# First two weight units unit by unit, later loads and clears reordered, last gate units by column halves

## What is computed

```
def reference(x, p, ...):
    h = x
    for i in range(DEPTH):                                  # DEPTH = 2
        h = h + 0.5 * swiglu(rmsnorm(h, ffn1_norm[i]), ffn1_w_gate[i], ffn1_w_up[i], ffn1_w_down[i])
        z = rmsnorm(h, mix_norm[i]) @ w_in[i]
        ...                                                 # short convolution and S5 scan over z give y
        h = h + y @ w_out[i]
        h = h + 0.5 * swiglu(rmsnorm(h, ffn2_norm[i]), ffn2_w_gate[i], ffn2_w_up[i], ffn2_w_down[i])
        gate = jax.nn.sigmoid(rmsnorm(h, ple_norm[i]) @ ple_w_gate[i])
        h = h + (p[i] @ ple_w_proj[i]) * gate
    return rmsnorm(h, final_norm)
```

## Times and profile before

| what | us |
|---|---|
| three executions | 1086.29, 1085.98, 1090.78 |
| their median | 1086.29 |
| the profiled execution | 1091.05 |
| its span in the trace | 1089.2 |
| TensorE busy | 1050.0 (96%) |
| VectorE busy | 675.1 (62%) |
| ScalarE busy | 513.1 (47%) |
| GpSimd busy | 408.0 (37%) |
| all TensorE waits for VectorE's `uL` (L933) | 10.9, in 2 places |
| TensorE waits for GpSimd's issue (L1296), at the start | 4.9, in 1 place |

### The profile page before, as it was taken

The page is one execution under the profiler, slowest core; times in us unless marked ns, Lnnn a source line. Parts: engine busy times, 40 slices in busy tenths (PEclk is TensorE's granted clock), DMA queues, the critical chain, the costliest instruction groups (busy, mean ns, idle before and its releaser), DMA issues.

```text
span 1089.2 us, 15176 instructions
## 1 busy us (share of the span) xinstructions
PE 1050.0 (96%) x5353; PEld 897.4 (82%) x5353; DVE 675.1 (62%) x772; ACT 513.1 (47%) x696; POOL 408.0 (37%) x605
## 2 busy tenths in 40 slices
PE   6999999999979999999999999999997999999996
PEld 5888888899877888888878888889997888888885
DVE  4555666468976555764777555546698765545464
ACT  4544444473364444444564444435535544444453
POOL 5888999314415888970029300001071100000000
PEclk9999999988989999999999999999798999999998
DMA  9655555241335955555536555552323465555541
GB/s 271 209 181 190 193 193 181 90 158 75 116 103 171 259 191 171 189 195 190 187 123 212 195 180 186 192 192 77 117 78 104 149 211 193 193 190 184 185 156 39
DMA packets 143385, 181.55 MB, mean 167 GB/s; under 512 B 18352, under 2 KB 125552, under 8 KB 143344
## 3 DMA queue, kind: packets, MB, share of 16 engines
q1 hardware_dynamic: 143200, 180.48, 50.3%
q10 hardware_dynamic: 144, 0.52, 0.1%
HBM read 179.93 MB, written 1.05 MB: 166 GB/s over the span
## 4 chain that ended last, share of the span: by engine, by line
PE 84%; DVE 11%; ACT 2%; issue 1%; SPq 1%; DMA 0%; POOL 0%; POOLq 0%; DVEq 0%; ACTq 0%
PE ps L1333 26%; PE ps L1335 26%; PE ps L1334 25%; DVE wL L706 2%; PE ps L1435 2%; PE ps L1345 1%; PE ps L1574 1%; PE ps L1575 1%; DVE regT L848 1%; ACT bufB L550 1%; DVE regT L835 1%; DVE bufA L871 1%; DVE regE L843 1%; PE ps L1451 1%; DVE uL L854 1%
## 5 line engine op out<-in xcount | busy, mean ns | idle before, releaser
L706 DVE TENSOR_TENSOR wL<-raw,wH 128x1024 fp32r<-128x1024 f32 x336 | 429.3, 1320 | 137.8 <-ACT wH L396 137.4
L396 ACT ACTIVATE wH<-raw 128x1024 fp32r<-128x1024 f32 x336 | 335.4, 1051 | 169.1 <-PE ps L1335 161.7
L1333 PE MATMUL ps<-wH,uH 128*128 128x512 f32 x832 | 330.2, 397 | 3.0 <-DVE uL L733 1.6
L1335 PE MATMUL ps<-wH,uL 128*128 128x512 f32 x832 | 324.6, 390 | 0.0
L1334 PE MATMUL ps<-wL,uH 128*128 128x512 f32 x832 | 324.4, 390 | 0.0
L1333 PEld LDWEIGHTS ps<-wH,uH 128*128 128x128 f32 x832 | 156.5, 188 | 36.0 <-DVE uL L733 3.6
L1335 PEld LDWEIGHTS ps<-wH,uL 128*128 128x128 f32 x832 | 156.3, 188 | 33.2
L1334 PEld LDWEIGHTS ps<-wL,uH 128*128 128x128 f32 x832 | 156.6, 188 | 30.8
L1068 POOL TENSOR_SCALAR ms<-ssq 128x2 f32<-128x2 f32 x8 | 4.5, 566 | 439.2 <-ACT bufB L410 409.7
L1333 PE MATMUL ps<-wH,hTH 128*128 128x512 f32 x352 | 140.1, 398 | 0.0
L1335 PE MATMUL ps<-wH,hTL 128*128 128x512 f32 x352 | 137.6, 391 | 0.0
(11 more groups left out here) (172 smaller groups left out, 1232.1 us busy)
## 6 DMA issues: line engine op xcount, KB each, us to landing
raw<-in_ffn_w_down_dram SPq DMA_DIRECT2D x88, 512.0 KB, 3.9
raw<-in_ffn_w_gate_dram SPq DMA_DIRECT2D x87, 512.0 KB, 4.0
raw<-in_ffn_w_up_dram SPq DMA_DIRECT2D x87, 512.0 KB, 5.0
raw<-in_w_in_dram SPq DMA_DIRECT2D x32, 512.0 KB, 4.3
raw<-in_w_out_dram SPq DMA_DIRECT2D x16, 512.0 KB, 4.0
raw<-in_ple_w_gate_dram SPq DMA_DIRECT2D x16, 512.0 KB, 3.7
raw<-in_glu_w_dram SPq DMA_DIRECT2D x4, 512.0 KB, 3.6
raw<-in_ple_w_proj_dram SPq DMA_DIRECT2D x4, 512.0 KB, 3.8
```

What stands on the lines that cost most here:

```text
L396: nc.scalar.activation(wH[:, slot, w], raw[:, slot, w], ACT.Copy).then_inc(wh_done, 1)
L706: nc.vector.tensor_tensor(wL[:, slot, w], raw[:, slot, w], wH[:, slot, w].bitcast(F32), ALU.subtract).then_inc((wl_half, wl_done)[a], 1)
L1333: mul(o, sH, vH, start=start, stop=False)
L1335: return mul(o, sL, vH, start=False, stop=stop)
```

## The change

1. **Start, TensorE.** In layer 0, tile 1 of x is transposed right behind tile 0, on its load's own semaphore, with six more warming products after it. Then unit 0 is used for both tiles, then unit 1 for both (`very_first_gate_up`), then the vectors are transposed.
2. **Start, VectorE and ScalarE.** The quarters are normed in the order 0, 2, 1, 3 (`norm_turn`). VectorE splits both halves of unit 0 behind quarter 0, and the halves of unit 1 around the rest of quarter 3; ScalarE splits unit 1 after all four quarters. The split of unit 2 comes ahead of the first silu.
3. **Start, loads and clears.** Tile 1 of x is loaded by SyncE, ahead of the second half of unit 0. The couplings are issued behind unit 4 instead of ahead of unit 3. GpSimd clears `regE` first, `Gr` and `Gi` behind the loads of x, `taps` and the vectors' step behind the first inverse norm.
4. **Parameters, both layers.** The three groups of `turn_params` stand together between the two tiles of unit 3, in PSUM banks 7, 2 and 3, without a wait between them; TensorE waits for all their copies ahead of unit 4.
5. **End.** In the last layer tile 1 uses gate units 2 and 3 for columns 0 to 511 first, then for 512 to 1023. `weighted` is done by quarter between the other steps, one of GpSimd's three steps of the last inverse root is made ahead, and ScalarE issues the store of the half that it scales.

```
@@ SyncE
+            sp.dma_start(xres[:, 1, :], x[0, P:2 * P, :]).then_inc(x_ld[1], 16)
...
-                    (lambda: (vectors(0), couplings(0))) if l == 0 else None)
+                    (lambda: vectors(0)) if l == 0 else None, None, (lambda: couplings(0)) if l == 0 else None)
@@ ScalarE, ffn
-                silus(l, f, 0, base + 1, between)
+                if l + f == 0:
+                    split_at(0, 2)
+                    silus(0, 0, 0, 1)
+                    vectors_turned(0, KD)
+                    split_at(0, 3)
+                else:
+                    silus(l, f, 0, base + 1, between)
                 if f == 0:
                     c_turned(l, 0)
                     c_turned(l, 1)
@@ ScalarE, embedding and finish
                     gate(3)
+                    finish(0)
                     last_squares(2)
                     last_squares(3)
+                    finish(1)
...
+                act.wait_ge(fin_act, t + 1)
+                act.dma_start(out[0, t * P:(t + 1) * P, 0:512], pp[:, t, 0:512]).then_inc(stored, 16)
@@ VectorE, embedding
-                    for t in range(NT):
-                        for q in range(2 * t, 2 * t + 2):
-                            gated(q)
-                            added(q)
-                        weighted(t)
+                    for q in range(4):
+                        gated(q)
+                        added(q)
+                        if q != 2:
+                            weighted(q)
+                        if q == 2:
+                            finish(0)
+                        if q == 3:
+                            weighted(2)
+                    finish(1)
@@ TensorE
+            def very_first_gate_up():
+                for part in range(2):
+                    for t in range(NT):
+                        pe.wait_ge(ul_done, 2 * part + t + 1)
+                        if t == 0:
+                            pe.wait_ge(wl_half, part + 1)
+                        gate_up_tile(part, part, t, (lambda n=part: take(0, n)) if t == 0 else None)
+                pe.wait_ge(pvt0_done, 1)
+                turn_vectors(0)
...
-                gate_up(l, base + 3, (base + 3) % SLOTS, 1)
+                take(l, base + 3)
+                gate_up_tile((base + 3) % SLOTS, 1, 0)
+                if f == 0:
+                    for which in range(3):
+                        turn_params(l, which)
+                gate_up_tile((base + 3) % SLOTS, 1, 1)
+                if f == 0:
+                    pe.wait_ge(ct_done, l * 4 + 4)
+                    pe.wait_ge(ptl_done, l + 2)
                 down(l, f, 0, base + 4, (base + 4) % SLOTS, first=True)
...
+                    for h in range(2):
+                        for j in (2, 3):
+                            for k in range(2):
...
+                                last = mm3(ps[:, ACC[2 + h], :], uH[at], uL[at], wH[:, slot, w], wL[:, slot, w],
+                                           False, j == 3 and k == 1)
+                        if h == 0:
+                            last.then_inc(last_half, 1)
```

More of the change, by code:

```diff
@@ L270, in gate_up, with ffn @@
                         for g, w in enumerate((wg, wu))]
-            def ffn(l, base, wg, wu, wd, then=None, later=None):
+            def ffn(l, base, wg, wu, wd, then=None, later=None, after=None):
                 def chunk(i, parts):
@@ L293, in ffn @@
                 back(1)
+                if after:
+                    after()
                 first = 2
@@ L367, in _ @@
             for t in range(NT):
-                sp.wait_ge(fin_act, t + 1)
-                sp.dma_start(out[0, t * P:(t + 1) * P, 0:512], pp[:, t, 0:512]).then_inc(stored, 16)
                 sp.wait_ge(fin_done, t + 1)
@@ L628, in gate @@
                         act.wait_ge(acc_t0, l * 5 + 5)
-                    if q == 2:
+                    if q == 2 and l + 1 == DEPTH:
+                        act.wait_ge(last_half, 1)
+                    elif q >= 2:
                         act.wait_ge(wt_used, used(l, U_GATE + 3))
@@ L685, in _ @@
                 embedding(l)
-            finish(0)
-            finish(1)
         @block.vector
@@ L783, in between @@
                     split_at(l, base + 3)
-                hidden(l, f, 0, between)
+                if l + f == 0:
+                    split_at(0, 2)
+                    hidden(0, 0, 0)
+                    split_at(0, 3)
+                else:
+                    hidden(l, f, 0, between)
                 if f == 0:
                     dve.wait_ge(pth_done, l + 1)
-                    nc.vector.tensor_tensor(pTL[:], ps[:, 7, :].rearrange("p (k n) -> p k n", k=2),
+                    nc.vector.tensor_tensor(pTL[:], ps[:, TURNED[2], :].rearrange("p (k n) -> p k n", k=2),
                                             pTH[:].bitcast(F32), ALU.subtract).then_inc(ptl_done, 1)
@@ L1024, in first_norm @@
                 half_split(0, 0, 0, 0)
+                half_split(0, 0, 0, 1)
+                gained(0, 0, 2)
                 gained(0, 0, 1)
-                half_split(0, 0, 0, 1)
+                rest(0, 0, 2)
                 rest(0, 0, 1)
-                split_at(0, 1)
-                half_norm(0, 0, 1)
+                gained(0, 0, 3)
+                half_split(0, 1, 1, 0)
+                rest(0, 0, 3)
+                half_split(0, 1, 1, 1)
             first_norm()
@@ L1304, in _ @@
                 if l == 0:
+                    clear_tables(taps)
+                    spread_steps(0)
                     setup_E(l)
@@ L1460, in turn_params @@
                         pe.wait_ge(bc_ld, (l + 1) * (16 * NBC))
-                    else:
-                        pe.wait_ge(ct_done, l * 4 + 2)
+                        pe.wait_ge(tg_done, l * 16 + 4)
                     for q in range(4):
-                        last = nc.tensor.transpose(ps[:, 7, q * P:(q + 1) * P],
+                        last = nc.tensor.transpose(ps[:, TURNED[which], q * P:(q + 1) * P],
                                                    cnat[:, which, q, :, :].rearrange("p d c -> p (d c)"), ident[:])
@@ L1467, in turn_params @@
                 else:
-                    pe.wait_ge(ct_done, l * 4 + 4)
                     for k in range(2):
                         for t in range(NT):
-                            last = nc.tensor.transpose(ps[:, 7, k * SEQ + t * P:k * SEQ + (t + 1) * P],
+                            last = nc.tensor.transpose(ps[:, TURNED[which], k * SEQ + t * P:k * SEQ + (t + 1) * P],
                                                        pnat[:, t, k * P:(k + 1) * P], ident[:])
@@ L1476, in ffn @@
                 base = FFN_BASE[f]
-                first_gate_up(l, f)
-                if f == 0:
-                    turn_params(l, 0)
+                if l + f == 0:
+                    very_first_gate_up()
+                else:
+                    first_gate_up(l, f)
                 take(l, base + 2)
@@ L1652, in _ @@
             turn_x(0, 0, 1)
+            warm(6)
+            turn_x(0, 0, 2)
+            turn_x(0, 0, 3)
             warm(6)
```

88 lines of the change are left out of this document (46 added, 42 removed).

## The result

The changed kernel takes **1094.97 us** (median of 20 runs, 1090.11 to 1096.48) where the kernel before takes 1086.78 (20 runs, 1085.51 to 1092.22): 1.0054 times as long over all runs, 95% interval 1.004 to 1.0068 (the two medians alone would give 1.0075, for a reason that the next paragraph shows). It is slower, and above the range of the prediction. The profiled execution took 1096.08 (span 1094.3), 5.0 more than that of before (1091.05, span 1089.2).

What follows compares the result with a forecast made beforehand. TensorE, 84% of the last-ending chain, was taken as the bound. 3.1 + 0.8 - 2.8 - 1.6 = -0.5, so 0.5 us slower; against the median 1086.29 that made 1086.8 us, range 1082.5 to 1091.0.

Steps and rivals of the forecast that it cites:

- the clock counted once: Behind the new waits at unit 4: TensorE falls to 1.2 GHz after one of the two, costing 1.6 us.
- Part 1: First two weight units, layer 0: tile 1 taken earlier, so TensorE is free for unit 2 at 23.66, 5.5 us earlier.
- Part 2, layer 0: Late parameter copies delay unit 4's split: new wait of 2.4 us, unit 4 at 38.8 instead of 41.92, gain 3.1.
- Part 2, layer 1: Same wait at unit 4 with nothing gained ahead of it: loss of 2.8 us, between 2.4 and 3.1.
- Part 3: Kernel's end: one GpSimd step less and last outputs issued from two engines, together 0.8 us gained, between 0.4 and 1.5.
- (a): Rival: the wait for unit 4 does not show, layer 1 loses nothing, 1080.0 us; chance 10%.
- (b): Rival, start: tile 1 of x lands no sooner, at 10.9, and the clock may fall; 1091.5 us; chance 8%.
- (c): Rival: the clock falls after both new waits and stays down 6.8 us each, 1091.6 us; chance 5%.
- (d): Rival, start: the later-issued couplings loads land after 32.2, where TensorE wants them; 1088.3 us; chance 5%.

## Why the prediction was wrong

It had the place and kind of the new waits right: a wait at unit 4 in both layers, made by ScalarE's late copies, and a fall of the clock behind it. What failed are sizes and the base. By the profiles it lost 4.6 us on the terms of the sum (5.1 slower, not 0.5; level against level 3.6), above all on the clock counted once and on part 1, and some 4 on what the sum was set upon.

- **The clock, 1.6 us counted, twice that paid.** "I count one of the two" was the mis-sized term. In the profile it fell behind both waits (3.41 us each), and filling the waits gave 3.0 to 3.2 back. The prediction sorted waits by length, 2.19 us on one side and 1.36 on the other; the profile of before already had a row against that, the wait of 1.42 us at 237.25 with 13.6 us at half clock behind it. Nor does the same wait always do the same: of the five profiles with an unfilled wait at layer 0's unit 4 four have the fall (not that of x by ScalarE), of the four with one in layer 1 three have it (not that of the changed kernel with six products). The term is 1.7 or 3.4, and perhaps 0, from run to run.
- **Part 1, 5.5 us forecast, 3.9 measured at unit 2's first product.** It starts at 25.29 where 23.66 was forecast. The weights ahead of x in the queue landed at 7.12 (6.40 before), x at 8.64 instead of 7.8, the half at 10.16 instead of 9.2: I gave x the half's former landing time, but x is twice as large. That the weights ahead of it came later too speaks for a share that x takes of their transfer; no run separates this. The half's split began at 10.19 (9.25 forecast), unit 1's split on VectorE at 17.35 (16.45 forecast), and unit 1's products all came about 1 us later; the wait of 1.16 us ahead of them was itself forecast (1.4). A wait of 0.43 for the hidden rows, forecast as just in time, is most of the rest. Part of the miss is this one execution's: the profiles of the six other versions with the same start (x loaded by SyncE ahead of the half) have this first product at 24.39 to 25.00, a gain of 4.2 to 4.8 us.
- **Part 2, layer 0: wait 2.4 forecast, 2.60 measured.** Behind 25.29 come 8.71 us to the first transpose (8.52), 0.63 to the copies (0.64), 2.59 to the split (2.5), 1.09 to VectorE's, 2.51 from there to TensorE's first product on unit 4 (2.34): the chain was read rightly, 0.4 short. With the later start unit 4 is at 40.82, not 38.8: a gain of 1.1 instead of 3.1.
- **Part 2, layer 1: 2.8 forecast (2.4 to 3.1), 3.18 measured.** The slow splits were forecast as likely (6.03 us for four). By the rule that the prediction took from the Trainium skill (SBUF — State Buffer, Who interferes with whom) the loss was to be the upper 3.1; the trace agrees. In layer 0 GpSimd had table steps under the same splits too, but of 16 columns: there VectorE kept its pace (4.65 us for four), and four of GpSimd's steps took 1.05 to 1.27 us each, which took 0.20 to 0.23 before and after.
- **Part 3, 0.8 forecast, 0.46 measured.** The last addition starts 7.42 us behind the first gated step (7.3 forecast, 7.43 before); from it to the span's end are 6.4 us instead of 6.8. Timeline of the changed kernel's last steps:

```profile
1080.51 0.69 DVE L987 SCALAR_TENSOR_TENSOR bufA<-bufB,bufA 128x512 f32<-128x512 f32 x1 [7.36 <-ACT bufB L644]
...
1087.93 0.69 DVE L994 TENSOR_TENSOR xres<-xres,bufA 128x512 f32<-128x512 f32 x1
...
1089.54 0.47 POOL L1344 TENSOR_TENSOR ms<-ms,ssqf 128x1 f32<-128x1 f32 x1 [1.50 <-ACT vv L419]
...
1090.67 0.72 ACT L687 ACTIVATE bufA<-bufA,rs 128x512 f32<-128x512 f32 x1 [1.29 <-POOL rs L1345]
1091.42 0.34 ACTq L689 DMA_DIRECT2D out_dram<-bufA  x1
```

- **The comparison.** The sum was made against a profiled run at the upper level and set on a median at the lower one. I saw the 4.8 us between the two and read them as spread. By its own steps the forecast for the upper level would have been 1091.5, and the measured 1095.3 would have been 3.7 off. Runs that come in two heaps ask for a forecast and a range around each. Why 14 of 20 runs are at the upper level after the change and 8 of 20 before is open.

The rivals: (a) was near as a price (1080.8 at the lower level once the groups are early) and wrong as a forecast; (b) happened only when forced, its fall of the clock included; (c) had two falls, which came, but of 3.4 us each and not of 6.8 (by its own numbers, half of 6.8 twice, it should have read 1092.0); (d) did not occur, the couplings landed at 31.98 and were wanted at 34.0.

## What to carry to other kernels

When TensorE's program gives another engine its work later, look for what stands behind that work in the other engine's order: here four copies held back a weight split, and a start 4 us faster brought 1. A wait of the matrix engine can cost more through its clock than its own length tells: here up to 1.7 us behind waits of 2.6 and 3.0 us, and 4.7 behind one of 1.42 us with small products after it; idle products under the wait are a cheap remedy, if they stand ahead of the very semaphore that is waited for and are shorter than the wait. And if a kernel's own runs fall into two heaps, find the stretch that differs before predicting anything smaller than their distance.

## What the runs showed of the hardware

A wait of 1.42 us, followed by 32 products of 64 columns, was followed by 13.65 us at a granted clock of 0.5 in some executions and not in others, 4.7 us of the kernel's time in layer 0; with idle products under the wait it was in none of six profiles, and the six runs of the kernel before with these products, and the six of the version with early groups, lie within 0.9 us each. Three later versions with them spread over 1.9 us (two of them) and 3.1 us, and the changed kernel with them over 4.9. After waits of 3.02 and 3.03 us at layer 1's unit 4 the clock fell in three profiles and not in a fourth, after waits of 2.60 to 2.65 us at layer 0's in four and not in a fifth. The Trainium skill says (TensorE: Matmul & The Clock Gate, What's actually happening) that how many products run at the lower level at a kernel's start differs between runs of the same kernel; these runs show that the same goes for the middle of a kernel.
